# Gate column blocks of the first projection moved between the units of the following stages, samples in column groups, expert turns spread anew

## The chip, the cores and the metric

The kernel runs on one core of a Trainium2 chip. The metric is the time of one launch in microseconds (us) of device time. The core's engines each have their own instruction stream and meet at semaphores: PE (TensorE), DVE (VectorE), ACT (ScalarE), POOL (GpSimd), and SP, which here only issues DMAs.

## The reference

One layer of a decoder step for 1024 prompt tokens and 8 x 4 sample tokens, width 1024, all in fp32:

```python
n1 = rms_norm(x, norm1_w) * (1 + sc1) + sh1
h = n1 @ w_in            # 1024 x 8704: q|f|i|g of the recurrence, q|k|v of 12 heads, 2 x 1024 gate logits
f = lb + (1 - lb) * sigmoid(fa)
oa, S_new = hgrn_chunked(qa, 1 - f, ia, log(f), S0)        # 4 heads, 128x128 state
ya = (rms_norm(oa, hgrn_norm_w) * silu(ga)) @ w_branch_a
ob = merge over 3 groups of dilated window attention (q and k normed, partly rotated)
yb = ob @ w_branch_b
gate_a, gate_b = split(sigmoid(gl))                        # gl: the gate logits
x = x + g1 * ((gate_a * ya + gate_b * yb) @ w_out)
n2 = rms_norm(x, norm2_w) * (1 + sc2) + sh2
x = x + g2 * peer(n2)    # 8 heads pick 16 of 16384 experts each; rows of u and v are gathered
```

The gate logits gl are needed by nothing before the sum with gate_a and gate_b.

## The kernel before

The tokens go through the front of the layer in two spans. The first, "_p", has 512 prompt tokens and nothing beside it but the modulation (c @ w_ada). The second, "_q", has 512 prompt tokens and the 32 sample tokens, and runs beside the expert stage of tokens that are through already. What is left of the experts follows alone (`experts_rest`). A span's front is a chain of stages with a barrier behind each: norm, projection, recurrence (`hgrn_phase`), attention, merge, branch, out, norm, query.

**Projection** (`project_phase`). The 8704 columns of w_in are 17 blocks of 512, in order: 2 T, 1 R, 1 T, 6 QK, 3 R, 4 T (the gates). A block is a number of units, each one accumulation in PSUM that ACT or VectorE brings to a stage tile and SP stores to DRAM (three slots in turn). In a T block a unit is 128 columns of w_in as stationary operand with the tokens moving (result transposed); in an R or QK block a unit is one tile of tokens as stationary operand with 512 columns of weights moving. The first span multiplies with split operands (`split`): POOL makes w_hi, a cast to fp32r of the raw weights, and w_lo, the difference, in two halves of 128x2048 per block, and each unit is 3 x 8 matmuls of 128x512. `raw` has two halves, w_hi and w_lo two buffers. The second span multiplies fp32 in 8 matmuls per unit; its sample tile has 32 tokens, so its stationary operand has 32 columns.

**Recurrence** (`hgrn_phase`). Four tiles of 128 tokens in a span (and the samples in the second). For a tile, ACT makes silu, sigmoid (`gates_in`), logs and exponentials, VectorE the forget gates, scans and products (`forgets`, `sums_of_logs`, `scaled`); PE turns the keys and forms the scores (`turn_keys`), then goes chunk by chunk through four chunks. The next tile's preparation is woven in. PE's order at the end of a tile is: sums of squares, `turn_keys(n + 1)`, then it waits for `rows_copied`.

**Attention and merge.** 12 jobs of 128 queries; in the second span 24 loads of past keys and as many of past values for the samples, in groups of four 32-column matmuls on four column groups. The merge weighs three groups' results on VectorE and PE turns the result.

**Order of the work beside.** Each engine calls `beside.pe(cost)` and its like at the same places of a stage. `Beside` adds cost x pace x rate to what is due and issues the expert turns (one turn is one part: 2 x 1 MB gathered by POOL's queue, a product on VectorE, weights on ACT, 8 matmuls on PE) that have fallen due. The rate is (242 - 24)/FRONT_US, the pace comes from `PACE` by stage. All 242 turns have to be issued by the end of the second front. In the first span `beside` is `Alone`, which does nothing; its projection has the modulation's turns.

**Norm.** `measure` squares a tile's rows on ACT with the sum of squares as accumulator output, and writes the squares over the tile `weight`; so it waits for `gains_done`, after which VectorE has read the weight.

## Time and profile before

| | |
|---|---|
| median of 3 runs | 4941.35 us (4936.12 to 4949.61) |
| the profiled execution | 4949.85 us |
| its span, first to last instruction | 4948.1 us |
| PE busy / DVE busy | 3458.2 us (70%) / 2607.4 us (53%) |
| ACT busy / POOL busy | 1961.7 us (40%) / 1468.3 us (30%) |
| mean DMA rate | 293 GB/s |
| granted TensorE clock, mean | 0.804 of 2.4 GHz |

The stages of the span can be told by their tiles: the first span's projection runs from 104 to 509 us, its recurrence from 513 to 675, attention from 676, merge from 786, branch from 815; the second span's projection from 1311 to 2082, recurrence to 2400, attention to 2645, merge to 2962; the experts alone from 3430. PE busy is the union of matmuls, which overlap; POOL busy in the second half is the issue of gathers.

### The profile page before, as it was taken

How to read it: one execution, taken by the hardware profiler on the slowest of the kernel's cores; microseconds unless marked ns; L12 is line 12 of the kernel's file. 1: busy time of each engine (PE TensorE's matmuls, PEld its weight loads, DVE VectorE, ACT ScalarE, POOL GpSimd, SP SyncE). 2: the span in 40 equal slices, each digit the busy share in tenths (PEclk: the TensorE clock that was granted, in tenths of full speed). 3: DMA queues.
4: the chain of work that ended last, by engine and by line, in shares of the span. 5: the costliest groups of instructions: out<-in, count | busy, mean ns of one | idle time of the engine just before them, and what ended most of it. 6: DMA issues, size and time to landing. Idle time of an engine off the chain costs nothing. (4 is left out here: it accounts for less than half of the span.)

```text
span 4948.1 us, 46668 instructions
## 1 busy us (share of the span) xinstructions
PE 3458.2 (70%) x14171; PEld 1808.8 (37%) x14171; DVE 2607.4 (53%) x6562; ACT 1961.7 (40%) x6734; POOL 1468.3 (30%) x1167
## 2 busy tenths in 40 slices
PE   4999676676599899878665448698555555555556
PEld 2778563563353234545442225365111111111111
DVE  2270333336446554366555763434766676767765
ACT  1121322024437653354443332323554554545554
POOL 2455000044221222212122230112444444444443
PEclk7999567788799999956787778798776777777778
DMA  5533124359787888856798997555999999999998
GB/s 190 212 130 133 43 83 127 117 183 375 274 334 285 306 326 329 295 175 255 272 374 325 400 424 250 217 192 204 417 411 406 406 420 398 420 397 417 414 411 365
DMA packets 310302, 1448.90 MB, mean 293 GB/s; under 512 B 40417, under 2 KB 100737, under 8 KB 161698
## 3 DMA queue, kind: packets, MB, share of 16 engines
q0 software_dynamic: 152064, 1107.36, 55.9%
q1 hardware_dynamic: 143618, 331.34, 19.0%
q10 hardware_dynamic: 14368, 7.21, 0.5%
q8 instruction: 112, 1.84, 0.1%
q14 instruction: 140, 1.15, 0.1%
HBM read 1378.41 MB, written 74.57 MB: 294 GB/s over the span
## 5 line engine op out<-in xcount | busy, mean ns | idle before, releaser
L2164 POOL DMA_INDIRECT uv_ring<-in_peer_uv,pick_idx x1056 | 1191.9, 1129 | 2645.8 <-PE expert_acc L2332 1835.5
L2332 PE MATMUL expert_acc<-uv_ring,diag 128*64 128x512 f32 x4096 | 1344.4, 793 | 714.3 <-ACT diag L2302 693.3
L2260 DVE SCALAR_TENSOR_TENSOR uv_ring<-uv_ring,n_pairs 128x1024 f32<-128x1024 f32 x1056 | 1280.5, 1226 | 797.7 <-DMA uv_ring<-in_peer_uv,pick_idx 771.6
L2332 PEld LDWEIGHTS expert_acc<-uv_ring,diag 128*64 128x64 f32 x4096 | 307.6, 167 | 1647.8 <-ACT diag L2302 1117.7
L2289 ACT ACTIVATE gelu_cube<-dots_now 128x2 f32<-128x2 f32 x528 | 105.8, 200 | 934.7 <-DVE uv_ring L2260 899.0
L558 PE MATMUL h_acc_q<-in_w_all_q,n_all_q 128*128 128x512 f32 (+1 forms) x800 | 358.2, 601 | 0.0
L2297 ACT ACTIVATE pick_weight<-gelu_tanh,pick_share 128x1 f32<-128x1 f32 x1056 | 350.9, 379 | 17.6
L2302 ACT ACTIVATE diag<-half_pattern,pick_weight 128x64 f32<-128x64 f32 x1024 | 300.4, 340 | 16.6
L2292 ACT ACTIVATE gelu_tanh<-gelu_cube,dots_now 128x1 f32<-128x1 f32 x1056 | 253.2, 286 | 16.0
L2294 ACT ACTIVATE pick_share<-dots_now,pick_prob 128x1 f32<-128x1 f32 x1056 | 245.3, 279 | 0.0
L555 PE MATMUL h_acc_q<-n_all_q,in_w_all_q 128*128 128x272 f32 x896 | 217.1, 400 | 13.2 <-DMA in_w_all_q<-in_w_in 13.2
L558 PEld LDWEIGHTS h_acc_q<-in_w_all_q,n_all_q 128*128 128x128 f32 (+1 forms) x800 | 135.8, 175 | 223.7 <-issue 223.7
L555 PEld LDWEIGHTS h_acc_q<-n_all_q,in_w_all_q 128*128 128x128 f32 x896 | 169.3, 192 | 74.9 <-issue 26.8
L1802 POOL CAST wq_hi_p<-wq_raw_p 128x1024 fp32r<-128x1024 f32 x16 | 17.0, 1065 | 541.0 <-DMA wq_raw_p<-in_peer_wq 527.4
L2290 ACT ACTIVATE gelu_cube<-gelu_cube,gelu_a 128x2 f32<-128x2 f32 x528 | 156.1, 296 | 17.2
L481 POOL TENSOR_TENSOR in_w_lo_p<-in_w_p,in_w_hi_p 128x2048 fp32r<-128x2048 f32 x34 | 156.0, 4589 | 2.7
L508 ACT COPY h_stage_q<-h_acc_q 128x272 f32<-128x272 f32 (+2 forms) x76 | 33.4, 439 | 292.1 <-PE h_acc_q L555 180.7
L480 POOL CAST in_w_hi_p<-in_w_p 128x2048 fp32r<-128x2048 f32 x34 | 64.4, 1895 | 261.5 <-DMA in_w_p<-in_w_in 255.5
L558 PE MATMUL h_acc_p<-in_w_lo_p,n_hi_p 128*128 128x512 f32 x320 | 126.3, 395 | 11.0 <-DVE h_stage_p L538 9.0
L1835 PE MATMUL peer_q_acc_q<-n_all_q,wq_raw_q 128*128 128x272 f32 x512 | 131.1, 418 | 2.6 <-DMA wq_raw_q<-in_peer_wq 2.6
L508 ACT COPY h_stage_p<-h_acc_p 128x512 f32<-128x512 f32 x44 | 25.9, 589 | 251.9 <-PE h_acc_p L555 169.4
L558 PE MATMUL h_acc_p<-in_w_hi_p,n_hi_p 128*128 128x512 f32 x320 | 125.3, 392 | 0.0
(418 smaller groups left out, 4972.8 us busy)
## 6 DMA issues: line engine op xcount, KB each, us to landing
in_w_p<-in_w_in SPq DMA_DIRECT2D x34, 1024.0 KB, 8.6
in_w_all_q<-in_w_in SPq DMA_DIRECT2D x17, 2048.0 KB, 10.5
ada_w<-in_w_ada SPq DMA_DIRECT2D x12, 2048.0 KB, 8.0
uv_ring<-in_peer_uv,pick_idx POOLq DMA_INDIRECT x1056, 14.1
past_keys_q<-in_past_keys SPq DMA_DIRECT2D x16, 1024.0 KB
past_rows_q<-in_past_values SPq DMA_DIRECT2D x16, 1024.0 KB, 8.8
score_pair<-scores SPq DMA_DIRECT2D x66, 128.0 KB, 7.0
wq_raw_p<-in_peer_wq SPq DMA_DIRECT2D x16, 512.0 KB, 4.8
```

The source lines that it names most:

```text
L481: nc.gpsimd.tensor_tensor(w_lo[:, n % 2, c], raw[:, half], w_hi[:, n % 2, c].bitcast(F32), ALU.subtract).then_inc(split_done, 1)
L555: ins = nc.tensor.matmul(acc[:, s, 0:k], w_part[:, b, c, at * P:(at + 1) * P], n_part[:, c, t0:t0 + k], start=start, stop=stop)
L558: ins = nc.tensor.matmul(acc[0:k, s, 0:WB], n_part[:, c, at * P:at * P + k], w_part[:, b, c, :], start=start, stop=stop)
L1835: ins = nc.tensor.matmul(acc[:, v % SLOTS, 0:n], w_part[:, u % 2, c, :], n_part[:, c, t0:t0 + n], start=(c == 0 and e == 0), stop=(c == DC ...
L2164: pool.indirect_dma_start(self.ring[:, 2 * slot + s, :], None, self.x["peer_uv"][0], bass.IndirectOffsetOnAxis(ap=self.idx[:, q % 2, s, k: ...
L2260: ins = dve.scalar_tensor_tensor(out=row, in0=row, scalar=1.0, in1=self.n2[:, tile % 2, s if tile < LAST_TILE else 0, :], op0=ALU.mult, op ...
L2290: link(act.activation(self.cube[:], self.cube[:], ACT.Identity, bias=self.const["gelu_a"][:], scale=GELU_B))
L2292: act.activation(self.tanh[:, s:s + 1], self.cube[:, s:s + 1], ACT.Tanh, scale=dots[:, s:s + 1])
L2294: ins = act.activation(self.share[:, s:s + 1], dots[:, s:s + 1], ACT.Copy, scale=self.prob[:, q % 2, k, s:s + 1])
L2297: ins = act.activation(self.weight[:, s:s + 1], self.tanh[:, s:s + 1], ACT.Identity, bias=self.share[:, s:s + 1], scale=self.share[:, s:s ...
L2302: ins = act.activation(self.diag[:, part % DIAGS, s, 0:pattern.shape[1]], pattern[:], ACT.Copy, scale=self.weight[:, s:s + 1])
L2332: ins = pe.matmul(self.acc[s * 64:(s + 1) * 64, c, :], self.diag[:, part % DIAGS, s, :], rows, start=first, stop=last)
```

## The change

1. The projection of the first span leaves out its last four blocks (the gates). `GateBlocks` does them as 16 single units, each 24 matmuls of 128x512, in the stages behind: `InGaps` gives one turn to an engine at each `beside.gap(name, turns)`. PE has 4 turns at the start of the recurrence and one at the end of each of its four tiles, 2 at the start of attention, 2 at the start of the merge, one in each of its four tiles and 2 at its end, 18 in all for 16 units. ACT copies a unit one turn later, SP stores it one turn after that; SP loads and POOL splits the next block meanwhile. The first gate block is still loaded and split inside the projection (`LOADED`). The operands n1 and the split weights are held until the merge's end. In the second span the gaps do nothing.
2. In the second span a sample unit of an R or QK block becomes four matmuls of 128 columns per chunk, one for each head's columns, on the four groups of 32 columns, so that the result lies on 128 partitions by 128 columns. Square, root, rotation and copy work on that shape; the store is four DMAs. Its cost counts as 128 columns.
3. `measure` writes its squares to a tile of its own, and ACT's wait for `gains_done` is gone.
4. `PACE` is 1.8 for the projection (was 1.46), 1.7 for attention (1.8), 1.25 for the merge (1.56); FRONT_US is 2010.0 (2006.3).

```diff
-    weight = sb("norm_weight", [P, D])
+    weight, squares = sb("norm_weight", [P, D]), sb("norm_squares", [P, D])
...
-            order.link(nc.scalar.activation(weight[0:w, :], of_rows(n, w), ACT.Square, accum_out=stat[0:w, n % 2, 0:1]))
+            order.link(nc.scalar.activation(squares[0:w, :], of_rows(n, w), ACT.Square, accum_out=stat[0:w, n % 2, 0:1]))
...
-        act.wait_ge(gains_done, 1)
...
+class GateBlocks:
+    BLOCKS = 4
+    PER = BLOCK // P
+    UNITS = BLOCKS * PER
+    TURNS = UNITS + 2
+    def __init__(self, nc, keep, bank, span, weights, n_hi, n_lo, x, dram):
+        self.nc, self.span, self.n_hi, self.n_lo, self.dram = nc, span, n_hi, n_lo, dram
+        self.raw, self.w_hi, self.w_lo = weights
+        sem = lambda name: nc.alloc_semaphore(name="gates_" + name)
+        self.stage = keep("gates_stage", [P, 2, BLOCK])
+        self.acc = bank("gates_acc", [P, 2, BLOCK])
+        self.raw_in = [sem("w0_loaded"), sem("w1_loaded")]
+        self.split_own, self.split_done, self.unit_done, self.staged = sem("split_own"), sem("split_done"), sem("unit_done"), sem("staged")
+        self.stored = [sem("stored0"), sem("stored1")]
+        self.order = Order(nc.gpsimd, self.split_own)
+        self.w_dram = x["w_in"]
+        self.before = len(column_blocks(BLOCK)) - self.BLOCKS
+    def load(self, k, half):
+        if k < self.BLOCKS:
+            sp = self.nc.sync
+            part = slice(half * DC // 2, (half + 1) * DC // 2)
+            at_least(sp, self.split_done, 2 * (k - 2) + half + 1 if k >= 2 else 0)
+            sp.dma_start(self.raw[:, half], self.w_dram[self.before + k][:, part]).then_inc(self.raw_in[half], 16)
+    def sp(self, t):
+        sp = self.nc.sync
+        j, m = divmod(t, self.PER)
+        if t == 0:
+            self.load(1, 0)
+            self.load(1, 1)
+        if m % 2 and j < self.BLOCKS:
+            self.load(j + 2, m // 2)
+        u = t - 2
+        if 0 <= u < self.UNITS:
+            sp.wait_ge(self.staged, u + 1)
+            row = T_GATE + u * P
+            sp.dma_start(self.dram["h_t"][row:row + P, self.span.first:self.span.first + BLOCK], self.stage[:, u % 2, :]).then_inc(self.stored[u % 2], 16)
+        if t == self.TURNS - 1:
+            for s in range(2):
+                sp.wait_ge(self.stored[s], 16 * (self.UNITS // 2))
+    def pool(self, t):
+        j, m = divmod(t, self.PER)
+        k, half = j + 1, m // 2
+        if m % 2 or k >= self.BLOCKS:
+            return
+        pool, b = self.nc.gpsimd, (self.before + k) % 2
+        part = slice(half * DC // 2, (half + 1) * DC // 2)
+        at_least(pool, self.unit_done, self.PER * (k - 1))
+        pool.wait_ge(self.raw_in[half], 16 * k)
+        self.order.link(pool.tensor_copy(self.w_hi[:, b, part], self.raw[:, half]))
+        pool.tensor_tensor(self.w_lo[:, b, part], self.raw[:, half], self.w_hi[:, b, part].bitcast(F32), ALU.subtract).then_inc(self.split_done, 1)
+    def pe(self, t):
+        if t >= self.UNITS:
+            return
+        pe = self.nc.tensor
+        k, m = divmod(t, self.PER)
+        b = (self.before + k) % 2
+        at_least(pe, self.split_done, 2 * k)
+        at_least(pe, self.staged, t - 1)
+        for c in range(DC):
+            for w_part, n_part in ((self.w_lo, self.n_hi), (self.w_hi, self.n_lo), (self.w_hi, self.n_hi)):
+                ins = pe.matmul(self.acc[:, t % 2, :], w_part[:, b, c, m * P:(m + 1) * P], n_part[:, c, :],
+                                start=(c == 0 and w_part is self.w_lo), stop=(c == DC - 1 and w_part is self.w_hi and n_part is self.n_hi))
+        ins.then_inc(self.unit_done, 1)
+    def act(self, t):
+        u = t - 1
+        if 0 <= u < self.UNITS:
+            act = self.nc.scalar
+            act.wait_ge(self.unit_done, u + 1)
+            at_least(act, self.stored[u % 2], 16 * (u // 2))
+            act.copy(self.stage[:, u % 2, :], self.acc[:, u % 2, :]).then_inc(self.staged, 1)
+def project_phase(nc, ph, span, beside, const, n_hi, n_lo, split_weights, ahead, x, consts, dram):
...
+    all_blocks = len(blocks)
+    blocks = blocks[:all_blocks - ahead]
+    LOADED = min(all_blocks, len(blocks) + 1)
...
+    row_cost = lambda w: COST * DC * (WB if w == P else P) * 0.00046
     units_of = [[(m, t0, k, COST * DC * max(0.11, k * 0.00046)) for m in range(WB // P) for t0, k in span.pieces] if kind == "T" else
-                [(n, at, w, COST * DC * max(0.11, WB * 0.00046)) for n, w, at in tiles] for _, kind, _ in blocks]
+                [(n, at, w, row_cost(w)) for n, w, at in tiles] for _, kind, _ in blocks]
     first = [sum(len(v) for v in units_of[:n]) for n in range(len(blocks) + 1)]
+    sample_unit = lambda kind, k: kind != "T" and k == S_TOK
+    stores = [NH if sample_unit(kind, unit[2]) else 1 for n, (_, kind, _) in enumerate(blocks) for unit in units_of[n]]
+    stores_in = lambda s, r: 16 * sum(stores[s:r * SLOTS:SLOTS])
...
+            for h in range(P // w):
+                sp.dma_start(rot[h * w:(h + 1) * w, n].rearrange("p a b -> p (a b)"), consts["rot"][at:at + w, :]).then_inc(consts_in, 16)
...
+                elif k == S_TOK:
+                    for h in range(NH):
+                        sp.dma_start(dram["qk" if kind == "QK" else "h_r"][t0:t0 + k, to + h * DH:to + (h + 1) * DH],
+                                     stage[h * k:(h + 1) * k, s, 0:DH]).then_inc(stored[s], 16)
...
+                heads = 1 if k == S_TOK else NH
                 if kind == "QK":
-                    for h in range(NH):
-                        ins = nc.scalar.activation(square[0:k, h, :], acc[0:k, s, h * DH:(h + 1) * DH], ACT.Square,
-                                                   accum_out=sums[0:k, s, h:h + 1])
+                    for h in range(heads):
+                        ins = nc.scalar.activation(square[:, h, :], acc[:, s, h * DH:(h + 1) * DH], ACT.Square,
...
+                    if sample_unit(kind, k):
+                        for h in range(NH):
+                            ins = nc.tensor.matmul(acc[h * k:(h + 1) * k, s, 0:DH], n_hi[:, c, at * P:at * P + k], w_all[:, b, c, h * DH:(h + 1) * DH],
+                                                   start=(c == 0), stop=(c == DC - 1))
+                        continue
...
             sp.dma_start(state_in[:].rearrange("p b h v -> p (b h) v"), st_dram).then_inc(s_in, 16)
+        load(1)
+        beside.gap("sp", 4)
         for n, w, at in tiles:
-            load(n + 1)
+            if n:
+                load(n + 1)
...
         gates_in(0)
+        beside.gap("act", 1)
         logs(0)
         exps(0)
+        beside.gap("act", 1)
         for n, w, at in tiles:
...
+        beside.gap("pe", 4)
         turn_keys(0)
         for n, w, at in span.full:
             s = n % 2
...
             turn_keys(n + 1)
             beside.pe(cost(n) * 0.2)
+            beside.gap("pe", 1)
...
+        beside.gap("pe", 2)
         if pairs:
             turn_queries()
         score(0)
...
+        beside.gap("pe", 2)
         for n in range(N):
             if span.samples:
                 for i in range(n * PER, (n + 1) * PER):
                     add_value(i)
                     beside.pe(COST_S / PER)
+            beside.gap("pe", 1)
...
             beside.pe(COST)
+        beside.gap("pe", 2)
...
+class InGaps(Alone):
+    def __init__(self, other):
+        self.turn = {"pe": other.pe, "act": other.act, "pool": other.pool, "sp": other.sp}
+        self.taken = {name: 0 for name in self.turn}
+    def gap(self, name, turns):
+        for _ in range(turns):
+            self.turn[name](self.taken[name])
+            self.taken[name] += 1
...
-PACE = {norm_phase: 1.2, project_phase: 1.46, hgrn_phase: 1.5, attention_phase: 1.8, merge_phase: 1.56, branch_phase: 1.2, out_phase: 1.2,
+PACE = {norm_phase: 1.2, project_phase: 1.8, hgrn_phase: 1.5, attention_phase: 1.7, merge_phase: 1.25, branch_phase: 1.2, out_phase: 1.2,
...
-FRONT_US = 2006.3
+FRONT_US = 2010.0
...
+                            if span.split:
+                                split_weights = (held(gated, "in_w", [P, 2, DC // 2, BLOCK]),
+                                                 held(gated, "in_w_hi", [P, 2, DC, BLOCK], F32R), held(gated, "in_w_lo", [P, 2, DC, BLOCK], F32R))
+                                ahead = GateBlocks.BLOCKS
+                            phase(project_phase, tag, busy, span, second, const, n_hi, n_lo, split_weights, ahead, x, consts, dram)
+                            assert busy or all(n == Modulation.TURNS for n in second.taken.values()), second.taken
+                        if span.split:
+                            here = lambda name, shape: gated.enter_context(nc.sbuf_tensor(name, shape, F32))
+                            banks = lambda name, shape: gated.enter_context(nc.psum_tensor(name, shape, F32))
+                            between = InGaps(GateBlocks(nc, here, banks, span, split_weights, n_hi, n_lo, x, dram))
+                        else:
+                            gated.close()
+                        o_a = held(early, "o_a", [P, HEADS, T], side="right")
+                        phase(hgrn_phase, tag, busy, span, between, const, x, consts, dram, state, o_a, state_p, state_s)
+                        with ExitStack() as scored:
+                            q_s, s_rows = held(scored, "q_sample_t", [P, G * HEADS, S_TOK]), held(scored, "past_scores", [P, G, P])
```

## Rows read from the trace of the kernel before

**Rows 1.** Windows: the last stretch, experts alone (busy us, instructions, clock, DMA).

```profile
3430.00:4948.00 1518.00, 873.57 (x2342) 192.86 (x2342) 1023.62 (x2527) 763.09 (x2951) 661.50 (x568) 0.74 0.99 404
```

**Rows 2.** Windows, first half: end of projection, recurrence, merge.

```profile
422.00:509.00 87.00, 87.00 (x386) 71.94 (x384) 0.00 (x0) 9.42 (x16) 38.84 (x12) 1.00 0.34 121
...
513.00:534.40 21.40, 0.00 (x0) 0.00 (x0) 9.15 (x33) 13.53 (x16) 0.00 (x0) 0.53 0.38 104
...
534.40:565.00 30.60, 28.65 (x170) 23.97 (x170) 13.26 (x44) 8.85 (x12) 0.00 (x0) 0.50 0.00 1
...
785.30:815.00 29.70, 4.46 (x16) 2.86 (x16) 20.16 (x52) 0.86 (x5) 0.00 (x0) 0.50 0.33 108
```

**Rows 3.** First half's projection: its first matmul (tile view), then ACT's timeline.

```profile
L555 PE MATMUL h_acc_p<-n_hi_p,in_w_lo_p x224: 389/389/794, 103.9 to 508.4; 128*128 128x512 f32 x112
...
111.63 0.59 ACT L508 COPY h_stage_p<-h_acc_p 128x512 f32<-128x512 f32 x1 [36.37 <-PE h_acc_p L555]
...
422.29 0.59 ACT L508 COPY h_stage_p<-h_acc_p 128x512 f32<-128x512 f32 x1 [4.85 <-PE h_acc_p L558]
...
509.32 0.59 ACT L508 COPY h_stage_p<-h_acc_p 128x512 f32<-128x512 f32 x1 [4.85 <-PE h_acc_p L555]
```

**Rows 4.** Timeline of PE in the recurrence; in brackets idle time and its releaser.

```profile
534.43 1.12 PE L861 MATMUL k_turned_p<-ident,cum_end_p 128*128 128x128 f32 x4 [25.14 <-DVE e_k_p L782]
...
570.09 2.45 PE L850 MATMUL state_update_p<-v_in_p,k_rows_p 32*128 32x128 f32 x13 [5.05 <-DVE attn_p L798]
```

**Rows 5.** Timelines of VectorE, then POOL, in the first half's projection.

```profile
242.25 1.13 DVE L526 SCALAR_TENSOR_TENSOR h_stage_p<-h_acc_p,qk_roots_p,qk_weights_p 128x128 f32<-128x128 f32 x4
...
243.41 4.65 DVE L533 TENSOR_TENSOR rot_parts_p<-h_stage_p,rot_rows_p 128x64 f32<-128x64 f32 x1
...
247.99 1.91 DVE L534 TENSOR_TENSOR rot_parts_p<-h_stage_p,rot_rows_p 128x64 f32<-128x64 f32 x1
...
241.42 1.90 POOL L480 CAST in_w_hi_p<-in_w_p 128x2048 fp32r<-128x2048 f32 x1 [14.84 <-DMA in_w_p<-in_w_in]
...
243.40 4.58 POOL L481 TENSOR_TENSOR in_w_lo_p<-in_w_p,in_w_hi_p 128x2048 fp32r<-128x2048 f32 x1
```

**Rows 6.** Timelines: starts of attention and merge, first half.

```profile
676.15 0.33 SPq L1024 DMA_DIRECT2D q_raw_p<-qk_rows_dram  x1
...
680.67 1.11 PE L1082 MATMUL att_turned_p<-ident,q_raw_p 128*128 128x128 f32 x4 [11.02 <-DMA k_raw_p<-qk_rows_dram]
...
786.31 16.26 SPq L1335 DMA_DIRECT2D att_parts_p<-att  x12
...
796.39 1.12 PE L1501 MATMUL ob_turned_p<-ident,merged_p 128*128 128x128 f32 x4 [14.78 <-DVE merged_p L1389]
...
812.43 1.11 PE L1501 MATMUL ob_turned_p<-ident,merged_p 128*128 128x128 f32 x4 [4.43 <-DVE merged_p L1389]
```

**Rows 7.** Timeline of VectorE in the first norm.

```profile
64.92 0.16 DVE L349 RECIPROCAL norm_stat_p<-norm_stat_p 128x1 f32<-128x1 f32 x1 [2.90 <-ACT norm_stat_p L317]
```

**Rows 8.** Windows, second half: projection, attention, merge.

```profile
1311.00:2082.00 771.00, 742.86 (x2408) 349.41 (x2408) 380.91 (x1117) 379.58 (x1318) 183.66 (x176) 0.98 0.84 315
...
2400.00:2645.00 245.00, 168.12 (x1460) 113.40 (x1464) 145.14 (x340) 124.58 (x422) 56.44 (x50) 0.86 0.95 354
...
2645.00:2962.00 317.00, 154.56 (x1255) 63.33 (x1247) 201.11 (x512) 118.27 (x457) 100.25 (x90) 0.73 0.95 385
```

**Rows 9.** Groups: whole span by form; projection; then PE's timeline in the merge.

```profile
L558 PE MATMUL h_acc_q<-in_w_all_q,n_all_q 128*32 128x512 f32 x160 | 71.4, 599 | 0.0
...
L2332 PE MATMUL expert_acc<-uv_ring,diag 128*64 128x512 f32 x712 | 179.2, 625 | 25.2 <-ACT diag L2302 17.4 <-DVE expert_x L2243 7.8
...
2737.71 1.08 PE L1489 MATMUL summed_s_q<-past_rows_q,probs_spread_q 128*32 128x128 f32 x32
```

**Rows 10.** Windows: one T block of the second projection; the merge's steady part.

```profile
1440.00:1481.00 41.00, 41.00 (x168) 26.06 (x167) 9.40 (x19) 15.89 (x60) 10.63 (x11) 1.00 0.91 349
...
2730.00:2960.00 230.00, 121.69 (x1065) 51.78 (x1065) 158.44 (x401) 91.12 (x354) 74.55 (x68) 0.77 1.00 411
```

More of the change, by code:

```diff
@@ L474, in split @@
         def split(n, half):
-            if n >= len(blocks) or not span.split:
+            if n >= LOADED or not span.split:
                 return
@@ L515, in _ @@
         done = 0
-        dve.wait_ge(consts_in, 16 * (2 + NT))
+        dve.wait_ge(consts_in, 16 * (2 + sum(P // w for _, w, _ in tiles)))
         for n, (_, kind, to) in enumerate(blocks):
@@ L539, in _ @@
+                    nc.vector.tensor_tensor(x2, turns[:, 2, 0:heads], turns[:, 3, 0:heads], ALU.add).then_inc(staged[s], 1)
                 beside.dve(cost)
```

100 lines of the change are left out of this document (58 added, 42 removed).

## The prediction

> **What bounds the kernel now.** I read the windows by stage first, then timelines at the places of the edit. The span falls in three: the first half alone, the second half with 218 expert parts woven in, and the remaining 286 parts, 1518 us at a DMA share of 0.99 [rows 1], or 5.3 us a part. The change leaves the third piece alone: FRONT_PARTS stays 242. In the first half the projection sets its own time: 87 of 87 us of PE busy at full clock [rows 2], one unit ending every 5.44 us (16 intervals from 422.29 to 509.32) [rows 3]. The recurrence that follows is the opposite: at its start PE idles 21.4 us, inside its tiles the granted clock is 0.50 (1.2 GHz), and DMA and POOL are idle; the merge has PE busy 4.5 of 29.7 us [rows 2]. In the second half the limits differ by stage [rows 8]: the projection is PE-bound (743 of 771 us busy, DMA share 0.84), attention and merge are DMA-bound (0.95 each, in the merge's steady part 1.00 at 411 GB/s [rows 10]) while PE is half idle.
>
> **First half: what leaves the projection.** 16 units x 5.44 = **-87 us** [rows 3]. Their load and split leave too, but lay under PE.
>
> **Recurrence, first 4 units.** PE idles 25.1 us before turn_keys(0) [rows 4]. The first unit after an idle PE took 103.9 to 111.63 = 7.7 us [rows 3], the next three 5.44 each: 24.0 us, done some 2.5 us later than that wait ends. Nearly hidden. ACT copies unit 0 before it makes its first exponential, and unit 1 before the logs: about 2.5 us, inside the same wait.
>
> **Recurrence, the splits on POOL.** Here the cost lies. Block 1 and 2 are now loaded and split while VectorE works on the chain that PE waits for; the old place of these splits was beside a VectorE with nothing to do. [rows 5] show what happens when they meet: the 128x64 TENSOR_TENSOR with two SBUF inputs that starts at 243.41 takes 4.65 us, exactly until POOL's 4.58 us subtraction ends, and the next is held 1.91 us by the cast behind it; the four operations before them, whose input is in PSUM, take 1.13 us beside a running cast. So VectorE passes one or two SBUF-SBUF operations at each edge of a POOL instruction. A block is 2 x (1.90 + 4.58) = 13 us of POOL. Block 1 lands some 5 us after its issue near 520, so POOL runs about 526 to 539, just where VectorE has 4 scans, 8 subtractions, 4 copies and 4 products to do; block 2 (its split waits for unit 3, near 537) follows directly, to about 553. Some 20 operations at one or two per edge, 8 edges: turn_keys(0) comes near 553 instead of 534.4. I take **+18 us**. Bounds: +2.5 (no hold-up, only the units' own end) and +26 (all four halves in full).
> The rule for this is in the Trainium skill, "GPSIMD Engine Reference", section Key points: POOL shares its SBUF interfaces with VectorE and contends with instructions that have two SBUF inputs or use a 2-port mode. By it the single-input TENSOR_SCALARs here would be held as well, and the sum would go to the upper bound, +26; the trace shows it only for two inputs.
>
> **Recurrence, one unit per tile.** After turn_keys(n+1) PE idles 5.05 us until VectorE has copied the rows [rows 4]. The unit put there comes out of a 1.2 GHz stretch, so 7.7 rather than 5.4 us: +2.6 each for three tiles. The clock it leaves behind gives some of that back in the next state updates; I take **+5** for the three and **+1.5** for the fourth, which overlaps the tail of VectorE (head norm). Bounds -9 and +16 (at 1.2 GHz throughout, 10.9 us a unit). Waiting behind ACT's copies (0.59 us each): gates_in(n+1), which has slack here. SP's waits on "staged" stand before load(2), which waits for the tile anyway.
>
> **Attention.** Two units at its start: PE idles 11.0 us over the stage change, of which 4.5 us (676.15 to 680.67) lie behind the first load of the stage [rows 6]. Unit 7 runs into the end of the recurrence, so 10.9 us less that 4.5: **+6.5**. Block 3's split falls there too, where VectorE mostly reads PSUM: nothing; +4 if its two small TENSOR_SCALARs are caught.
>
> **Merge.** PE idles 14.8 us before its first transposes at 796.39; the first load is issued at 786.31, so I let PE start at 785.3 [rows 6]. Two units: 7.7 + 5.4, to 798.4; then four times unit and transposes, 5.4 + 1.1 = 6.5, to 824.4, plus a 0.7 us copy: 825.1 against 814.3, **+10.8**. PE replaces VectorE (796.39 to 812.43 over three tiles, 5.3 us each) as what sets this stage. Bounds +4 and +35 (all at 1.2 GHz).
>
> **Norms.** ACT's Square no longer waits for the gains. After the gains VectorE sits idle 2.90 us until the first root [rows 7], the same length in all four norm stages: 4 x 2.9 = **-11.6**. The Modulation turns come sooner (pace 1.8); their matmuls are the same and PE is still the bound: 0. The extra rot rows and stores of samples are SP issues of 0.3 us with SP not late: 0.
>
> **Second half, samples in column groups.** A sample unit is 8 matmuls, 16 records of 0.446 us (71.4 us over 160 records for the ten units): 7.14 us [rows 9]. It becomes 32 matmuls, 64 records, 128 columns each. The same form, four groups of 32 columns in turn, stands in the merge: 32 records in 1.08 us [rows 9]. So 2.16 us, and 10 x 4.98 = **-50 us** of PE in a PE-bound stage.
>
> **Turns spread anew.** Parts due are cost x pace x rate. The rate goes from 218/2006.3 = 0.10866 to 218/2010 = 0.10846. A T block costs 29.6, a row block 34.9 before (five units of 6.97) and 29.6 after (4 x 6.97 + 1.74). Projection: (7 x 29.6 + 10 x 34.9) x 1.46 x 0.10866 = 88.2 parts before (712 records/8 = 89 in the trace [rows 9]), 503.7 x 1.8 x 0.10846 = 98.3 after. Attention 28.2 to 26.6 (cost 144), merge 42.0 to 33.6 (cost 248). Ten parts move from DMA-bound stages to the PE-bound one. Each costs PE 179.2/89 = 2.0 us there: **+20**. Is there room on the DMA? Now 315 GB/s x 771 us = 243 MB; after, with 10.1 x 2.1 MB more, 264 MB in about 741 us: 356 GB/s, where a T block now runs at 349 with PE full [rows 10]. That is near the edge (share about 0.95), so I add **+3** for late landings. Projection: -27, to 744.
> Merge: 8.4 parts of 2.1 MB at 411 GB/s would be -43; the first quarter of the stage is its start-up, not saturated (385 GB/s over all of it [rows 8]), so **-38**. Attention: 1.6 parts x 2.1 MB / 354 GB/s = **-9**.
>
> **Sum.** First half: -87 + 18 + 6.5 + 6.5 + 10.8 = -45.2. Norms -11.6. Second half: -50 + 20 + 3 - 38 - 9 = -74. Together -131. The profiled execution took 4949.85 us (span 4948.1 and 1.75 around it), 8.5 above the median; the sum is a difference, so from the median 4941.35 it gives **4810**. What measurement can tell from no change is about 0.3%, 15 us.
>
> **Rivals.**
> (a) The clock wakes. In the recurrence PE runs 28.7 of 30.6 us at clock 0.50 [rows 2]; if the units kept it at 2.4 GHz, the 16 chunks' chains, some 4.5 us of PE each, would shorten by about a third: -30 more, **4780**. For it: the units are the densest work in the stage. Against: tiles are 30 us of thin matmuls between two units. The Trainium skill ("TensorE: Matmul & The Clock Gate", The HAM clock gate) has the clock released by activity and withdrawn without it; by that it would fall again inside each tile, as I assume.
> (b) Merge and attention are not DMA-bound in the sense needed: their own chains (VectorE in order, 201 of 317 us busy [rows 8]) hold them. They give back 15 instead of 47: **4842**.
> (c) The projection of the second half becomes DMA-bound. If 315 GB/s is what it can carry, 264 MB take 838 us: +67 instead of -27, **4904**. Against: 349 GB/s in one of its own blocks.
> (d) Column groups do not run side by side with 128 rows of contraction and this data: no -50, **4860**. Against: [rows 9].
> (e) Other side: the moved units are not hidden at all. If PE stays at 1.2 GHz and every unit lies on the path, 16 x 10.9 = 174, and all three blocks hold VectorE, 39: first half 174 + 39 - 87 - 6 = +120, second half -80: +40, **4981**, slower. It decides once the recurrence, attention and merge together grow by more than about 190 us (87 + 12 + 74 to break even); idle PE of 25, 11 and 15 us in front of them speaks against.
>
> **Numbers.** Forecast 0.60, (a) 0.11, (b) 0.15, (c) 0.08, (d) 0.03, (e) 0.03. The forecast's own bounds (hold-up 2.5 to 26, tiles, merge) make about 4785 to 4845; with (a) and (b) the range is 4770 to 4865. Faster by over 0.3%: 0.95; within: 0.02; slower: 0.03.
>
> **What would show it.** Projection of the first half 87 us shorter with the same 5.44 us beat; turn_keys(0) about 40 us after the recurrence's first instruction instead of 21.5, with single TENSOR_TENSORs or scans of 4.6 us in front of it; state_update waiting for PE, not VectorE; merge with PE as the releaser, 10 us longer; sample units near 2.2 us; second projection near 744 us with DMA share above 0.9, merge near 279, attention near 236. The prediction is wrong if the second projection does not shrink, or if turn_keys(0) is on time.

## The result and the profile after

The changed kernel takes 4878.3 us (median of 4 runs, 4868.7 to 4884.7) against 4944.9 for the kernel before beside it: a ratio of **0.986**, 95% interval 0.984 to 0.988. It is faster, as forecast, but by half of the forecast's 131 us, and outside its range. The profiled executions have spans of 4876.4 and 4948.1 us, 71.7 apart. "_p" in a name is the first half, "_q" the second.

First the windows of the changed kernel: the start of the recurrence, its first tile, the merge of the first half, then the second half's projection, attention and merge (they answer to [rows 2] and [rows 8]; stretches run from a stage's first matmul to its last, so they are a little shorter than those of before).

```profile
core 0: us, PE busy (x) PEld busy (x) DVE busy (x) ACT busy (x) POOL busy (x), PEclk, DMA share, GB/s
425.50:472.50 47.00, 23.65 (x96) 19.08 (x96) 32.72 (x33) 14.71 (x19) 26.17 (x8) 0.76 0.49 154
472.50:500.00 27.50, 25.57 (x133) 22.45 (x134) 12.60 (x43) 7.76 (x11) 0.00 (x0) 0.50 0.00 1
745.00:777.00 32.00, 25.54 (x120) 21.00 (x119) 15.52 (x37) 4.48 (x9) 0.00 (x0) 0.96 0.39 126
1263.40:2060.00 796.60, 731.47 (x2962) 358.69 (x2964) 413.89 (x1202) 386.70 (x1368) 211.86 (x196) 0.96 0.87 330
2370.00:2615.00 245.00, 165.11 (x1420) 110.61 (x1420) 137.07 (x327) 117.98 (x399) 50.80 (x46) 0.84 0.89 330
2615.00:2880.00 265.00, 132.72 (x1212) 59.92 (x1214) 168.56 (x419) 95.16 (x370) 75.84 (x71) 0.74 0.95 387
```

The fourth row holds the surprise. TensorE is busy 731 us instead of 743, as it should be with less work, yet from its first to its last matmul the stage is 30 us longer (796.1 against 765.8): TensorE waits 65 us. The DMA share is 0.87, so the transfers do not fill it. A part of the experts ends on TensorE as a **sum**: eight matmuls with `diag`, the weights that ACT has brought into shape, as stationary operand. What TensorE waits for is in the list of its waits over that stretch (total us, times, longest); the changed kernel first, then the first line of the same list of the kernel before, whose other two (the weights and expert_x) are 13.2 and 7.8 us, nearly the same:

```profile
PE expert_acc L2481 <- ACT diag L2451: 52.4, 15, 5.3
PE h_acc_q L657 <- DMA in_w_all_q<-in_w_in: 13.4, 1, 13.4
PE expert_acc L2481 <- DVE expert_x L2392: 8.2, 1, 8.2
PE h_acc_q L651 <- issue: 4.2, 13, 0.4
```

```profile
PE expert_acc L2332 <- ACT diag L2302: 17.4, 5, 4.9
```

Five waits for ACT's diag have become fifteen. The timeline of the changed kernel shows one, on TensorE and then on ACT:

```profile
1584.66 7.13 PE L660 MATMUL h_acc_q<-in_w_all_q,n_all_q 128*128 128x512 f32 x16
1591.72 1.94 PE L2481 MATMUL expert_acc<-uv_ring,diag 128*64 128x512 f32 x8
1598.54 3.68 PE L2481 MATMUL expert_acc<-uv_ring,diag 128*64 128x512 f32 x8 [4.88 <-ACT diag L2451]
1602.15 2.62 PE L651 MATMUL h_acc_q<-in_w_all_q,n_all_q 128*32 128x128 f32 x64
```

```profile
1591.83 0.28 ACT L596 ACTIVATE qk_square_q<-h_acc_q 128x128 f32<-128x128 f32 x1 [2.27 <-PE h_acc_q L660]
...
1592.99 1.28 ACT L599 ACT_TABLE_LOAD   x1
1594.28 0.30 ACT L599 ACTIVATE qk_roots_q<-qk_sums_q,eps 128x4 f32<-128x4 f32 x1
...
1595.02 1.28 ACT L2441 ACT_TABLE_LOAD   x1
1596.32 0.48 ACT L2441 ACTIVATE gelu_tanh<-gelu_cube,dots_now 128x1 f32<-128x1 f32 x2
...
1597.90 0.59 ACT L2451 ACTIVATE diag<-half_pattern,pick_weight 128x64 f32<-128x64 f32 x2
```

After a QK unit (ends 1591.7) two expert turns fall due at once. The first sum has its diag, made a turn ago. The second needs the one that ACT makes in this turn, and ACT comes to it only behind its own work for the unit: squares, a load of its table and the root, then a second load and the steps of the turn itself, 6.7 us from the end of the unit to the diag. TensorE stands 4.88 us, and the sum then takes 3.68 us instead of 1.94: the granted clock from 1598.5 to 1602.2 is 0.50 (1.2 GHz), before the wait it was 1.00. I call this a **double turn**. The rule by which parts fall due predicts them: a QK or row unit draws 6.97 x 1.8 x 0.10846 = 1.36 parts in the changed kernel and 6.97 x 1.46 x 0.10866 = 1.11 before; counted through the stage, 14 units take two turns against 5. The fifteenth wait stands behind a sample unit (1.27 us at 1654.06). Not all double turns cost the same: of the waits before, three are 4.8 to 4.9 us and two 1.4.

The recurrence's start. VectorE, then POOL and TensorE, in the changed kernel:

```profile
439.00 2.70 DVE L859 TENSOR_SCALAR forget_p<-forget_p,lb_rest_p,lb_p 128x128 f32<-128x128 f32 x4 [3.19 <-ACT forget_p L789]
441.73 4.86 DVE L863 TENSOR_SCALAR key_p<-forget_p 128x512 f32<-128x512 f32 x1
446.62 13.13 DVE L872 TENSOR_TENSOR_SCAN cum_p<-chunk_reset_p,logf_p 128x128 f32<-128x128 f32 x4
459.79 1.80 DVE L877 TENSOR_TENSOR cum_mid_p<-cum_p 128x128 f32<-128x128 f32 x1
461.50 0.28 DVE L878 TENSOR_TENSOR cum_end_p<-cum_p 128x128 f32<-128x128 f32 x1
461.71 4.58 DVE L877 TENSOR_TENSOR cum_mid_p<-cum_p 128x128 f32<-128x128 f32 x1
```

```profile
439.65 1.97 POOL L455 CAST in_w_hi_p<-in_w_p 128x2048 fp32r<-128x2048 f32 x1 [19.80 <-DMA in_w_p<-in_w_in]
...
461.52 4.62 POOL L456 TENSOR_TENSOR in_w_lo_p<-in_w_p,in_w_hi_p 128x2048 fp32r<-128x2048 f32 x1
```

```profile
472.51 1.11 PE L973 MATMUL k_turned_p<-ident,cum_end_p 128*128 128x128 f32 x4 [23.34 <-DVE e_k_p L894]
```

POOL works from 439.65 to 466.1, and VectorE passes hardly more than one operation at each of its edges, the single-input TENSOR_SCALAR at 441.73 among them. turn_keys(0) starts 51.2 us after the last matmul of the projection (421.3), which is 47 us after the recurrence's first matmul; in the kernel before it starts 25.5 us after the projection's last matmul (508.9) and is itself the first matmul of the recurrence [rows 4].

Stage by stage, from the same instruction in both traces (before minus after: the gain reached at that point; o_sums are the sums of squares that end a tile of the recurrence):

| point | gain, us |
|---|---|
| first matmul of the first projection | 1.3 |
| last matmul of the first projection | 87.6 |
| turn_keys(0), first half | 61.9 |
| last o_sums of the recurrence | 61.4 |
| first transposes of attention | 53.9 |
| first matmul of the branch | 41.7 |
| first matmul of the second projection | 47.6 |
| last matmul of the second projection | 17.3 |
| first / last transposes of attention_q | 22.9 / 24.2 |
| last transposes of merge_q | 67.8 |
| end | 71.7 |

### The profile page after: what moved, and what is told of

It is laid out like the page before. It is cut to its first block and busy times, and to the rows that moved or that the text cites. A ratio compares the mean times of both kernels' runs of the same rounds, so it can differ in the third digit from the quotient of the medians.

```text
span 4876.4 us, 47596 instructions
## 1 busy us (share of the span) xinstructions
PE 3401.8 (70%) x14651; PEld 1798.2 (37%) x14651; DVE 2624.7 (54%) x6544; ACT 1942.7 (40%) x6689; POOL 1495.1 (31%) x1167
## 3 DMA queue, kind: packets, MB, share of 16 engines
q1 hardware_dynamic: 145202, 331.36, 19.5%
## 5 line engine op out<-in xcount | busy, mean ns | idle before, releaser
L2313 POOL DMA_INDIRECT uv_ring<-in_peer_uv,pick_idx x1056 | 1217.5, 1153 | 2593.2 <-PE expert_acc L2481 1784.0
L660 PE MATMUL h_acc_q<-in_w_all_q,n_all_q 128*128 128x512 f32 x640 | 289.1, 605 | 0.0
L657 PE MATMUL h_acc_q<-n_all_q,in_w_all_q 128*128 128x272 f32 x896 | 219.1, 401 | 13.4 <-DMA in_w_all_q<-in_w_in 13.4
L660 PEld LDWEIGHTS h_acc_q<-in_w_all_q,n_all_q 128*128 128x128 f32 x640 | 120.1, 193 | 170.3 <-issue 170.2
L576 POOL TENSOR_TENSOR in_w_lo_p<-in_w_p,in_w_hi_p 128x2048 fp32r<-128x2048 f32 x28 | 128.5, 4588 | 2.2
L660 PE MATMUL h_acc_p<-in_w_hi_p,n_lo_p 128*128 128x512 f32 x320 | 126.0, 394 | 0.0
L575 POOL CAST in_w_hi_p<-in_w_p 128x2048 fp32r<-128x2048 f32 x28 | 53.2, 1899 | 234.9 <-DMA in_w_p<-in_w_in 223.1
L1965 PEld LDWEIGHTS peer_q_acc_q<-n_all_q,wq_raw_q 128*128 128x128 f32 x512 | 101.1, 200 | 24.9 <-DMA wq_raw_q<-in_peer_wq 2.9
```

The costliest lines, as they stand in the source:

```text
L576: nc.gpsimd.tensor_tensor(w_lo[:, n % 2, c], raw[:, half], w_hi[:, n % 2, c].bitcast(F32), ALU.subtract).then_inc(split_done, 1)
L657: ins = nc.tensor.matmul(acc[:, s, 0:k], w_part[:, b, c, at * P:(at + 1) * P], n_part[:, c, t0:t0 + k], start=start, stop=stop)
L660: ins = nc.tensor.matmul(acc[0:k, s, 0:WB], n_part[:, c, at * P:at * P + k], w_part[:, b, c, :], start=start, stop=stop)
L1965: ins = nc.tensor.matmul(acc[:, v % SLOTS, 0:n], w_part[:, u % 2, c, :], n_part[:, c, t0:t0 + n], start=(c == 0 and e == 0), stop=(c == DC ...
L2313: pool.indirect_dma_start(self.ring[:, 2 * slot + s, :], None, self.x["peer_uv"][0], bass.IndirectOffsetOnAxis(ap=self.idx[:, q % 2, s, k: ...
```

## The experiments

Thirteen kernels ran. "Projection" is the second half's, from its first to its last matmul: 765.8 us before, 796.1 in the changed kernel. Ratios are to the kernel before, with 95% intervals.

| kernel | ratio | projection, us | parts there | waits for diag, us (times) |
|---|---|---|---|---|
| before | 1 | 765.8 | 89 | 17.4 (5) |
| changed | 0.986 [0.984, 0.988] | 796.1 | 99 | 52.4 (15) |
| changed, parts per stage of before | 0.9868 [0.985, 0.989] | 749.0 | 89 | 32.4 (11) |
| changed, one turn a unit | 0.9747 [0.973, 0.977] | 747.6 | 99 | 14.2 (6) |
| changed, no root | 0.9789 [0.977, 0.981] | 761.7 | 99 | 28.9 (14) |
| before, one turn a unit | 0.9932 [0.991, 0.995] | 740.3 | 89 | 0 |
| before + column groups | 0.9953 [0.994, 0.997] | 735.6 | 89 | 18.1 (9) |
| the same, one turn a unit | 0.9927 [0.990, 0.995] | 718.5 | 89 | 18.4 (6) |
| the same, none after samples | 0.9862 [0.984, 0.989] | 690.0 | 88 | 0 |

**1. The parts of each stage as before.** The column groups, the moved units and the norms stay.

```
-PACE = {norm_phase: 1.2, project_phase: 1.8, hgrn_phase: 1.5, attention_phase: 1.7, merge_phase: 1.25, ...
+PACE = {norm_phase: 1.2, project_phase: 1.612, hgrn_phase: 1.5, attention_phase: 1.8, merge_phase: 1.56, ...
...
-FRONT_US = 2010.0
+FRONT_US = 2006.3
```

> The changed kernel with the expert parts per stage put back to those of before: 88 in the second projection (98 in the changed kernel), 28 in attention, 42 in merge. Theory (double turns): a QK or row unit now draws 1.22 parts, so about 9 of the 40 units take two turns, instead of 15. The second projection loses ten parts (10 x 2.1 = 21 us of TensorE) and some 6 waits for ACT's diag (6 x 3.5 = 21 us): 796 - 42 = about 754 us from its first to its last matmul; merge gives back what it had gained, about 45. Total within 10 us of the changed kernel, 4870 to 4890. Rival (the 57 us are lost to something else in that stage, the sample units or their stores): the projection stays above 775 us and the total rises to 4900 or more.

4880.1 us: the total did not move (0.9868 against 0.986), the projection fell by 47 us and attention and merge took 57 more (merge_q 308.8 us, 263.2 in the changed kernel). So the new spread was worth nothing: what it took from the merge it paid for in the projection, 4.7 us a part, where the forecast had 2.3.

**2. One turn a unit.** In the second projection no unit is followed by more than one turn; the rest stays due.

```
 def take(self, name, turn, us):
     self.due[name] += us * self.much * self.rate
-    while self.taken[name] < min(self.until, int(self.due[name] + 1e-3)):
+    end = self.taken[name] + self.most      # 1 in the second projection
+    while self.taken[name] < min(self.until, int(self.due[name] + 1e-3), end):
...
```

> The changed kernel, where in the second projection no unit is followed by more than one expert turn; what is due stays due and is taken after a later unit, so the parts of the stage stay 98. Theory (double turns): the waits of the weighted sums for ACT's diag, 15 with 52 us, fall to 5 or fewer with under 20 us, the projection shortens by 30 to 40 us and the total by as much: about 4840. Rival (transfers: the ring is full and every part lands late; or the part's own 2.1 us of TensorE at a lower clock): the waits move to the transfers' arrival and the total changes by less than 10 us.

4823.9 us, 54 less, more than the 30 to 40 expected; 48.5 of it in the projection, with the same 99 parts. TensorE's waits over the stage, and its window:

```profile
PE expert_acc L2482 <- ACT diag L2452: 14.2, 6, 7.0
...
PE h_acc_q L651 <- issue: 6.4, 20, 0.4
```

```profile
1266.20:2017.00 750.80, 721.90 (x2968) 355.08 (x2968) 413.20 (x1202) 398.64 (x1386) 209.47 (x196) 0.98 0.90 351
```

The transfers now run at 351 GB/s instead of 330: they had not been the limit. Waits for diag fell by 38 us, and the sums themselves from 210.3 to 198.9 us, since fewer follow a pause and run at 1.2 GHz. Five of the six waits that are left stand behind sample units.

**3. The same rule on the kernel before.**

> The kernel before, where in the second projection no unit is followed by more than one expert turn; nothing else. Theory (double turns): the kernel before has five of them, with 17.4 us of waits for ACT's diag and the sums behind them at 1.2 GHz; they go and the second projection shortens by 15 to 20 us, the total by as much (0.996 to 0.997). Rival (the rule gained 54 us on the changed kernel because it smooths the transfers, not because of double turns): 30 us or more here, or nothing.

4917.5 us, 0.9932, 32 under the kernel before beside it; projection 740.3, 25.5 less, no wait for diag left. Five double turns had cost the kernel before 5 us each on average, more than expected: the waits are 17.4 us, the sums fell from 179.2 to 173.8 us, and the rest is other work of TensorE at 1.2 GHz behind the waits (clock 0.98 to 0.99). The total of 32 us alone would also fit the rival, which asked for 30 or more. Against it stand the stage, where 22.8 of the 25.5 us are these waits and sums, and the transfers, whose wait (expert_x, 7.8 us) did not move; the other 7 us of the total lie outside the stage and are not explained.

**4. ACT's table loads taken away.** Is it ACT that is late?

```
-nc.scalar.activation(roots[...], sums[...], ACT.Sqrt, bias=const["eps"][:], ...
+nc.scalar.activation(roots[...], sums[...], ACT.Sqrt if span.split else ACT.Identity, bias=const["eps"][:], ...
```

> The changed kernel with Identity in the place of ACT's Sqrt in the second projection: what it leaves out is the square root of the QK norm there. The two loads of ACT's table (1.28 us each) go from each QK unit. Theory (the second sum of a double turn waits for the diag that ACT makes after its own work for the unit): some 9 of the 24 QK units take two turns, each gets 2.6 us back, the waits for diag fall from 52 us to about 30, and the total by 20 to 25 us. Rival (what is late in a double turn is the part's transfer or VectorE's product): the waits stay and the total moves by less than 6 us.

4842.7 us, 36 less, more than expected; 34 of it in the projection. Still 14 waits, but the longest is 2.6 us instead of 5.3:

```profile
PE expert_acc L2481 <- ACT diag L2451: 28.9, 14, 2.6
```

ACT has 52 instructions less in the stage and is busy 67 us less, 1.28 us for each, and the most frequent wait fell from 4.88 to 2.32 us, by just two loads. The number of waits is set by the double turns, their length by ACT's chain. VectorE's products and the transfers are what they were, so they were not what came last.

**5. The column groups alone.** project_phase of the changed kernel in the kernel before, with the costs of before.

> The kernel before, with the samples in column groups in the second projection and nothing else; parts per unit as before (1.1 a row unit, a sample unit still draws its own). Forecast's term: 10 x 4.98 = 50 us off the second projection, total 50 us under before (0.990). Theory of double turns: the same, since no unit draws more than before. Rival (the gain is eaten by the sample units' own chain, four stores and one sum on ACT and VectorE, or by transfers that now have less time): no more than 25 us.

4922.9 us; projection 735.6, a gain of 30 us, not 50. The total moved by 22, since attention and merge gave some back. So a second part of the miss lies here. Where the 20 us are, the trace tells. The ten sample units took 35 us, not the 21.6 of the forecast: 27.9 busy and 7.4 of gaps between the short matmuls (busy us, mean ns, idle time before them over the stage):

```profile
L569 PE MATMUL h_acc_q<-in_w_all_q,n_all_q 128*32 128x128 f32 x640 | 27.9, 277 | 7.5 <-issue 7.4
```

That is 14 us; 5 more are sums at 1.2 GHz (179.2 to 183.8), and the waits for diag are nearly what they were (17.4 to 18.1). So in this trace it is in the main the sample units that eat the gain, as the rival has it. But the next two experiments, where the same units take 19.5 us without a gap, show that being quick does not help while a turn stands behind them.

**6 and 7. The groups with one turn a unit, and with none after samples.** In the second of them a sample unit adds to what is due but is not followed by a turn.

```
+    row_cost = lambda w: COST * DC * max(0.11, WB * 0.00046) * (-1 if w == S_TOK else 1)
...
+        self.due[name] += abs(us) * self.much * self.rate
+        if us < 0:
+            return
```

> The kernel before with the column groups of the samples and with one turn a unit in the second projection (89 parts, as before). Groups alone gave 30 us in that stage, one turn a unit alone 25. Theory (a sample unit of 3 us is followed by a turn for which ACT needs 6 us, so TensorE waits for its diag there too): the 5 double turns go, the waits behind the sample units stay; projection 715 to 722 us. Rival (the groups' missing 20 us were the double turns): 766 - 50 - 19 = 697 us.

> As the one before, but no turn follows a sample unit; what falls due there is taken after later units (89 parts in 96 units). Theory (waits behind the sample units): the waits for diag in the stage fall to under 3 us and the projection is 5 to 12 us shorter than with turns after the samples. Rival (the sample units are long for reasons of their own, the gaps in the issue of 64 matmuls): the same within 4 us.

718.5 and 690.0 us: 28.5 us between them, far more than the 5 to 12 expected. Nearly all of it is 18.4 us of waits for diag and 9.1 us of sums (181.4 to 172.2, one part less). TensorE in the first, then in the second:

```profile
1502.88 1.94 PE L2353 MATMUL expert_acc<-uv_ring,diag 128*64 128x512 f32 x8
1504.75 1.95 PE L569 MATMUL h_acc_q<-in_w_all_q,n_all_q 128*32 128x128 f32 x64
1509.69 1.94 PE L2353 MATMUL expert_acc<-uv_ring,diag 128*64 128x512 f32 x8 [2.99 <-ACT diag L2323]
```

```profile
1503.87 1.94 PE L2355 MATMUL expert_acc<-uv_ring,diag 128*64 128x512 f32 x8
1505.74 1.95 PE L569 MATMUL h_acc_q<-in_w_all_q,n_all_q 128*32 128x128 f32 x64
1507.62 2.84 PE L578 MATMUL h_acc_q<-in_w_all_q,n_all_q 128*128 128x512 f32 x6
```

Between two sums TensorE now has 1.95 us of work, while ACT is still at the chain of the QK unit before (its diag is ready at 1509.65). The old sample unit of 7.14 us had covered that chain. Against the kernel before with one turn a unit, 740.3, the last one is 50.3 us shorter, some 48 if the one part that fell outside its stage (88 instead of 89) is added at 2 us: **near the forecast's 50 us, once nothing waits behind the short units**.

**8. The splits cut away.** POOL's two instructions for each half of blocks 1 to 3 work on 2 columns instead of 512, which leaves out nearly all of that splitting.

```
-pool.tensor_copy(self.w_hi[:, b, part], self.raw[:, half])
+pool.tensor_copy(self.w_hi[:, b, part, 0:2], self.raw[:, half, :, 0:2])
...                                                # the subtraction likewise
```

> The changed kernel with POOL's split of the gates' blocks 1 to 3 cut from 512 columns to 2 in each instruction: what it leaves out is nearly all of the splitting of these weights, the loads, the waits and the 16 units stand. Theory (hold-up of VectorE beside POOL): turn_keys(0) starts 24 us after the recurrence's first matmul instead of 47, no VectorE instruction there takes 4.6 us, and the total falls by 20 to 26 us. Rival (the units themselves delay the chain, through ACT's copies or TensorE): turn_keys(0) stays above 40 us and the total moves by less than 5 us.

4840.1 us. turn_keys(0) starts at 450.43, 22 us earlier, and VectorE's same instructions read:

```profile
439.67 1.12 DVE L859 TENSOR_SCALAR forget_p<-forget_p,lb_rest_p,lb_p 128x128 f32<-128x128 f32 x4 [3.19 <-ACT forget_p L789]
440.82 0.43 DVE L863 TENSOR_SCALAR key_p<-forget_p 128x512 f32<-128x512 f32 x1
442.08 1.37 DVE L872 TENSOR_TENSOR_SCAN cum_p<-chunk_reset_p,logf_p 128x128 f32<-128x128 f32 x4 [0.83 <-ACT logf_p L796]
```

Added up against the changed kernel: 1.6 + 4.4 + 11.8 + 1.5 + 4.3 = 23.6 us of hold-up. The total fell by 38, though; 24 of it is there at the start of the second projection. The other 14 come piecemeal in attention, merge and the third piece, where both kernels have the same code; stages of the second half differ by 5 to 10 us between kernels that are alike there, and I assign them to nothing.

**9. The splits later.** POOL waits for what turn_keys(n) waits for before it splits.

```
+pool.wait_ge(scaled_done, 1)               # before gap("pool", 4)
...
+pool.wait_ge(scaled_done, min(n + 2, N))   # before the gap of tile n
```

> The changed kernel, where POOL waits, before it splits the gates' block 1, for the signal that turn_keys(0) waits for, and before the gap of tile n for that of turn_keys(n + 1); all work is done. Theory (hold-up of VectorE is dear only where TensorE waits for VectorE): turn_keys(0) comes 24 us after the first matmul of the recurrence instead of 47; the splits then lie beside the tiles, where VectorE has some slack, and give back up to 8 us. Total 14 to 22 us under the changed kernel, near 4860. Rival (it only moves: the same eight edges hold the scans of the next tile): less than 8 us gained.

4856.0 us (0.9818 [0.980, 0.984]), 22 less. turn_keys(0) comes at 447.9, and the splits beside the first tiles give 7.7 us back (from turn_keys(0) to the last o_sums 142.4 us, 134.7 in the changed kernel). All work is done in this one.

**10 to 13. Both mends, and where the parts go.** Four kernels with one turn a unit and the late splits; the last one takes no turn after samples, counts a T unit 1.4 times and has 93 parts in the projection.

> The changed kernel with both mends and its own paces: one turn a unit in the second projection (alone -54 us) and the late splits (alone -20). They lie in different halves: if they add, 4878 - 54 - 20 = 4804; if the second half only gives back what comes earlier, no less than 4824.

> The changed kernel with both mends, one turn a unit in the second projection and the late splits, and with eight more parts moved from the merge into the projection (pace 1.95 and 0.97: 106 parts in 106 units, 26 in the merge). Theory: 4824 - 18 (late splits) - 8 x (5.2 of the merge - 1.5 of the projection) = about 4775. Rival (at 106 parts the projection's transfers are full, 264 MB + 17 MB in 765 us is 367 GB/s): parts land late, the projection grows by 15 us more and the total stays near 4800.

> As the kernel with both mends, with paces 1.87 and 1.12: 102 parts in the projection, the most that one turn a unit takes without a rest of two or more at its end, and 30 in the merge. The kernel with 106 due left 4.4 of them to the start of the recurrence, which grew by 21 us. Theory (that burst ate the gain): four parts moved at (5.2 - 1.5) us, 10 to 15 us under the kernel with the changed kernel's paces, about 4792. Rival (the projection's transfers are full at 98 parts already): no gain, 4804 or more.

> The changed kernel with both mends (one turn a unit, late splits) and no turn after a sample unit; so that 93 parts fit into the 96 other units, a T unit counts 1.4 times, the pace is 1.45 in the projection and 1.48 in the merge (39 to 40 parts). With one turn a unit alone the projection took 748 us for 98 parts; with the same rule on the kernel before, the step from turns after the samples to none gave 28 us. Theory (a turn behind a 3 us sample unit waits for ACT's diag, here as there): projection 690 + 4 x 2 = about 700 us; the merge gives 6 x 5.5 = 33 back, total about 4800. Rival (at the changed kernel's spread the transfers bound the stage, share 0.90): projection no shorter than 748 - 5 x 2 = 735, total 4835 or more.

| kernel | us (range) | ratio | projection | recurrence_q | merge_q |
|---|---|---|---|---|---|
| both mends, paces of the changed kernel | 4811.0 (4797 to 4820) | 0.9717 [0.969, 0.974] | 745.6 | 294.9 | 262.1 |
| 106 parts due | 4801.5 (4787 to 4805) | 0.9704 [0.969, 0.972] | 752.8 | 317.0 | 226.1 |
| 102 parts due | 4807.9 (4794 to 4825) | 0.9720 [0.970, 0.974] | 749.7 | 310.0 | 253.1 |
| none after samples, 93 parts | 4811.5 (4797 to 4815) | 0.9709 [0.969, 0.973] | 713.8 | 299.2 | 284.3 |

(Recurrence_q from the end of the projection to the last o_sums, merge_q from the last transposes of attention to its own.) The mends add, to within 9 us: 4878 - 54 - 22 = 4802, measured 4811. Moving more parts out of the merge gains nothing measurable: 106 due was expected to give 4775 and gave 4801.5, the total that its rival named, although the projection grew by 7 us (752.8 against 745.6) and not by 15; 102 due instead of 98 was expected to bring 10 to 15 us and brought 3, inside the noise. The recurrence took them. The recurrence sums 198 / 8 = 25 parts (eight matmuls each) in 295 us with the first kernel, 27.5 in 310 with 102 due and 31.5 in 317 with 106. The burst is the likely reason for 106 due, where 4.4 parts are left over at its end; with 102 due the 15 us are more than three parts explain, and that stays open.

The last kernel tests the waits behind sample units on the changed kernel: the projection falls to 713.8 us, against 700 expected by the theory and 735 by transfers as the limit. Not one wait for diag is left but 2.3 us; of the 14 above 700, 10 are slower sample units (25.7 us of them and 4.2 of gaps; 19.5 and none in experiments 6 and 7), the rest that wait and one part more. The parts that no longer fit went to the merge, which grew by 22 us; the total stayed at 4811 where 4800 was expected.

## Why the forecast was 68 us short

Against its own steps, for the profiled pair (71.7 us gained, 131 forecast):

- **Leaves the projection, -87:** right, 87.6 - 1.3 = 86.3. So the other 13 blocks kept their time.
- **Splits hold VectorE, +18:** 25.7 (87.6 - 61.9), 22 to 24 of it the hold-up. The upper bound, +26, was nearly right. I had read [rows 5] as a rule for two SBUF inputs; here the single-input TENSOR_SCALAR took 4.86 us beside POOL and 0.43 without. The Trainium skill ("GPSIMD Engine Reference", Key points) names instructions in a 2-port mode beside those with two SBUF inputs. By that the prediction had its +26, and the runs agree with it, though none of them shows the mode itself.
- **Tiles, +5; tail and attention, 1.5 + 6.5 = +8; merge, +10.8:** 0.5, 7.5 and 11.8. The three units in the tiles took 6.4, 5.7 and 5.7 us instead of 7.7, and the chunk behind each ran at 2.4 GHz, 2.42 us instead of 4.02. From one o_sums to the next it is 39.1, 37.4 and 30.0 us against 36.6, 36.5 and 32.9: in the first two tiles TensorE then waits for VectorE's state, 7.9 and 6.9 us instead of 3.6 and 3.5, and only in the last, where no next tile is made ready, the quick chunk is a gain. Rival (a) is thus true of one chunk in four: the three tiles with a unit have a mean clock of 0.63 to 0.67 instead of 0.50 to 0.55, the other chunks take 4.02 us as before, so the clock falls again inside each tile, as the prediction had assumed.
- **Norms, -11.6:** right: 1.3 us in the first norm, and TensorE's wait for the first transposes shorter by 2.9, 3.1 and 3.0 us in the other three, 10.3 in all.
- **Samples in column groups, -50:** the short matmuls can do what was computed, 19.5 us for ten units in three of the kernels (21.6 forecast). What failed is the word "PE-bound": at 1.95 us the unit is shorter than ACT's chain for the unit before, and a turn behind it waits. It gave -30 alone, -22 with one turn a unit (718.5 against 740.3), and -48 to -50 with none after samples. In the changed kernel the units also had gaps, 26.9 + 4.2 us.
- **Turns spread anew, "Each costs PE 179.2/89 = 2.0 us there: +20", and +3 for late landings: this step failed most.** It priced a part by TensorE's mean work. But the ten parts do not come one by one: a row unit's draw rises from 1.11 to 1.22 because a sample unit now counts less, and to 1.36 with the higher pace, and that takes the double turns from 5 to 14. Ten parts cost 47 us, not 23 (experiment 1). Of the stage's miss of 57 us, 20 is the groups' (experiment 5) and the rest the double turns and what goes with them. By steps of one change each: -30.2 for the groups (765.8 to 735.6), +13.4 for the lower cost of a sample unit, which gives the row units more to draw (735.6 to 749.0, waits for diag 18.1 to 32.4 us; the first halves of these two kernels differ as well), +47.1 for the ten parts (749.0 to 796.1). Such steps add up to +30.3 by themselves, so that they do is no proof, and the shares depend on the order: with double turns barred the groups give -21.8 and the ten parts +29.1, and allowing them costs 25.5 us before and 48.5 in the changed kernel.
- **Merge, -38:** -44; **attention, -9:** -1 in this pair. Over all kernels attention_q takes 245.7 to 255.7 us with 28 parts (six traces, mean 252) and 241 to 249 with 26.6 (nine, mean 244): -8 after all, and the pair happened to hide it.

Rival (d), 4860, comes nearest in time and is false in its reason: the groups do run side by side, 1.95 us a unit. Rival (c), 4904, is wrong in its mechanism: the transfers reached 351 GB/s as soon as the turns were spaced. Rival (b) gave 4842, but it was the merge that delivered and the projection that did not. Rival (e) was far off. The sign that the prediction itself had named for being wrong came true: the second projection did not shrink, it grew by 30 us.

All in all: most of the miss is waiting for an engine that was 49% busy, and the slower matmuls behind these waits. ACT stood in no list of limits, and I had not asked what it does between two turns.

## What to carry to other kernels

When work is woven in by shares, price it by the gap it falls into, not by its mean: list, for each engine, the time from one insertion to the next, and compare it with the longest chain that must run there. A quota that goes above one per gap, or a gap that a faster instruction makes short, turns hidden latency into a wait; a cap of one per gap cost a few lines and gave 54 us. And when a stage's unit is made faster, look for what its length had been hiding.

## What the runs showed that was not expected

- POOL's CAST and subtraction over 128x2048 hold VectorE's single-input TENSOR_SCALAR on f32: 4.86 us for 128x512 beside them, 0.43 alone; four scans 13.13 against 1.37.
- A pause of TensorE can cost twice. In the changed kernel's second projection each of the eleven pauses before a sum of 3.1 to 8.2 us was followed by eight matmuls of 3.2 to 3.7 us instead of 1.94, and each of the four of 1.44 us by 1.94. The length alone does not decide it: the fifteenth wait, 1.27 us, was followed by 3.02, and in experiment 6 five of the pauses are 2.99 us, and the sums behind them took 1.94 (clock 1.00) or 3.1 to 3.6 (clock 0.51 at 1552).
- A switch of ACT's table shows as 1.28 us and nothing around it; without 52 of them the second projection was 34 us shorter.
- The same 64 short matmuls of a sample unit run without a gap in some kernels (19.5 us for ten units) and with gaps of 0.3 to 1.2 us put down to issue in others (25 to 29 us, and 3 to 7 of gaps). It is not the order of the instructions in the stage: experiment 2 (29.2 and 6.4 us) and the first kernel of 10 to 13 (19.5 and none) differ only in where POOL splits in the first half. What decides it was not tried.
